# A two-block transformer layer on one core: z's projection moved into the delta rule's preparation, and the spatial mixing moved between the gates' projections

## The reference, cut to what matters

```python
mod_x = silu(c) @ ada_w + ada_b                     # six rows of 1024
hx = modulate(rms_norm(x, norm_mix_g), mod_x[0], mod_x[1])
x_qkv, x_beta, x_a, x_z, x_u, x_v, x_gates = split(hx @ w_in)   # z, u, v 1024 columns each, gates 2048
o_x = gated delta rule, both directions (x_qkv, x_beta, x_a, state of the context)
# gated_delta_chunked, for each chunk:
T = triangular_solve(eye + low, eye)                # inverse of a unit lower triangle
u = T @ (v * beta);  w = T @ (kb * exp(G))
v_new = u - w @ s;  o = q_dec @ s + qk @ v_new;  s = s * g_last + k_dec.T @ v_new
y_gdn = rms_norm(o_x, gdn_norm_g) * silu(x_z)
v = layer_norm(gelu(x_v), sgu_ln_g, sgu_ln_b)
y_sgu = gelu(x_u) * (w_s @ v + b_s)                 # 128x128 over positions, per group of 128 channels
g_a, g_b = sigmoid(x_gates)
x = x + mod_x[2] * ((g_a * (y_gdn @ w_a) + g_b * (y_sgu @ w_b)) @ w_out)
```

## Time and profile before

| | us |
|---|---|
| median of 3 timed executions | 1808.69 (1803.87 to 1810.02) |
| the profiled execution | 1803.05 |
| its span, first to last instruction | 1801.0 |
| TensorE busy in the span | 1518.5 (84%) |
| VectorE busy | 812.4 (45%) |
| ScalarE / GpSimd busy | 368.4 / 190.5 |
| mean granted clock of TensorE | 0.913 of full |

### The profile page before, as it was taken

One profiled execution on the slowest core, in us unless ns is written; L12 is line 12 of the kernel. 1 busy time (PEld: TensorE's weight loads), 2 busy tenths in 40 slices (PEclk: granted clock), 3 DMA queues, 4 the chain that ended last, 5 costly groups with the idle time before them and its releaser, 6 DMA issues. The chain is left out here.

```text
span 1801.0 us, 19500 instructions
## 1 busy us (share of the span) xinstructions
PE 1518.5 (84%) x7553; PEld 897.5 (50%) x7553; DVE 812.4 (45%) x1512; ACT 368.4 (20%) x698; POOL 190.5 (11%) x280
## 2 busy tenths in 40 slices
PE   4999964588999799465879895999889899999977
PEld 2877764578544344152324332444444447656573
DVE  2344648444254457632112114257474405566554
ACT  3221144111011100010001002100351124642230
POOL 0000016500000000001000000000251001213340
PEclk9899977567999999868989997999999999999998
DMA  9331002110677656469999995352602212121120
GB/s 350 92 94 47 1 1 48 42 34 10 234 269 264 249 215 228 154 250 419 411 384 373 411 371 174 98 182 70 187 1 70 94 47 94 47 94 47 49 70 24
DMA packets 132298, 283.60 MB, mean 157 GB/s; under 512 B 28744, under 2 KB 39272, under 8 KB 126955
## 3 DMA queue, kind: packets, MB, share of 16 engines
q1 hardware_dynamic: 128608, 266.65, 41.2%
q0 software_dynamic: 3600, 15.73, 2.1%
HBM read 312.77 MB, written 4.19 MB: 176 GB/s over the span
## 5 line engine op out<-in xcount | busy, mean ns | idle before, releaser
L1329 PE MATMUL ps<-ring,hTx 128*128 128x512 f32 x320 | 139.2, 593 | 1.9 <-PEq L176 1.8
L2641 PE MATMUL ps<-hT,ring 128*128 128x512 f32 x256 | 111.8, 593 | 3.1 <-PEq L2548 2.7
L316 DVE SCALAR_TENSOR_TENSOR ada_acc<-ring,cact,ada_acc 128x512 f32<-128x512 f32 x154 | 104.1, 745 | 0.5
L1329 PEld LDWEIGHTS ps<-ring,hTx 128*128 128x128 f32 x320 | 60.4, 190 | 77.1 <-issue 77.1
L620 PE MATMUL ps<-hTx,ring 128*128 128x256 f32 x384 | 91.1, 393 | 5.3 <-PEq L176 5.3
L2276 PE MATMUL ps<-hT,ring 128*128 128x512 f32 x208 | 90.4, 592 | 0.0
L620 PEld LDWEIGHTS ps<-hTx,ring 128*128 128x128 f32 x384 | 74.8, 197 | 19.7 <-issue 8.0
L2641 PEld LDWEIGHTS ps<-hT,ring 128*128 128x128 f32 x256 | 47.9, 190 | 60.9 <-issue 60.9
L1862 PE MATMUL ps<-ring,hTx 128*32 128x512 f32 x384 | 51.3, 683 | 26.6 <-DMA ring<-in_expert_w 26.6
L711 DVE SCALAR_TENSOR_TENSOR conv<-xpad,taps,conv 128x512 f32<-128x512 f32 (+1 forms) x96 | 63.6, 663 | 3.4
L2276 PEld LDWEIGHTS ps<-hT,ring 128*128 128x128 f32 x208 | 39.5, 190 | 48.5 <-issue 48.3
(11 more groups left out here) (522 smaller groups left out, 2680.3 us busy)
## 6 DMA issues: line engine op xcount, KB each, us to landing
ring<-in_expert_w SPq DMA_DIRECT2D x24, 2048.0 KB, 14.4
far<-in_expert_w SPq DMA_DIRECT2D x24, 2048.0 KB, 18.2
ring<-in_w_in SPq DMA_DIRECT2D x16, 2048.0 KB, 13.1
ring<-in_ada_w SPq DMA_DIRECT2D x12, 2048.0 KB, 9.2
ring<-in_w_ada SPq DMA_DIRECT2D x12, 2048.0 KB, 8.9
ring<-in_w_in_c SPq DMA_DIRECT2D x10, 2048.0 KB, 8.4
ring<-in_expert_w POOLq DMA_DIRECT2D x32, 512.0 KB
far<-in_expert_w POOLq DMA_DIRECT2D x32, 512.0 KB
```

The lines of the kernel that those rows point to most:

```text
L316: ins = dve.scalar_tensor_tensor(out=part, in0=slot[:, kt], scalar=c[:, kt:kt + 1], in1=part, op0=ALU.mult, op1=ALU.add)
L1329: ins = pe.matmul(ps[:, 2 + i % BANKS], hTx[:, kt, t * P:(t + 1) * P], stream.slot(n)[:, kt], start=(kt == 0), stop=(kt == KT - 1))
L2641: ins = pe.matmul(bank, slot[:, kt, j % 4 * P:(j % 4 + 1) * P], hT[:, kt], **edge)
```

## The change

z's two panels get a place of their own in the list, with lent panels between, and are projected in the preparation block, behind PE's last transposes; ScalarE applies Silu there, around its transposition of the solution. `zs` is allocated before the delta rule, and the state lies in `nt[:, 0]`, which is dead by then, in place of a tensor of its own. u's first panel is issued in the first scan block. In the projection stage the modulation's panels and those of `w_in` alternate from the start (eight pairs), so a modulation panel k stands in front of `w_in` panel k+1, and sum k comes behind projection k+1 as before, the last behind the last. DVE starts with the normalisation of `otok` and its product with `zs`, ahead of the first dot. The mixing block is gone: its matmuls run behind unit 12 of 16, the transposes of `otok` behind 13, those of `uu` behind 14, in banks 1, 5, 6 and 7, so the projections keep banks 2 to 4. Two lent panels behind the merge keep the experts' slots where they were. The diff, cut ("..." is left out):

```diff
-zuvg, rest = [], []
-for i in range(10):
-    zuvg.append(len(stream.panels))
+lend = lambda: add(lambda slot: [])
+z_in, gdn_lent = [], []
+for i in range(2):
+    z_in.append(len(stream.panels))
     add_cols(w_in, COL_Z + i * PANEL)
-    if 1 <= i < 9:
-        rest.append(len(stream.panels))
-        add_cols(ada, (3 + i) * PANEL)
+    for _ in range(RING - 1):
+        gdn_lent.append(len(stream.panels))
+        lend()
+uvg, rest = [], []
+for i in range(8):
+    uvg.append(len(stream.panels))
+    add_cols(w_in, COL_Z + (2 + i) * PANEL)
+    rest.append(len(stream.panels))
+    add_cols(ada, (4 + i) * PANEL)
...
+ffn_lent, ab_in = [], []
+for i in range(2):
+    ffn_lent.append(len(stream.panels))
+    lend()
...
-        state = sb(scope, "state", [P, UNITS, P])
+        state = nt[:, 0]
...
+                    stream.issue(sp, z_in[1] + 1)
                     store_solution(sp, 0)
                     load_solution(sp, 0)
...
                     turn(PAIRS - 1)
+                    pe.wait_ge(erowed, 2 * PAIRS)
+                    for i in range(2 * TT):
+                        n, t = z_in[i // TT], i % TT
+                        if t == 0:
+                            pe.wait_ge(*stream.arrive(n))
+                        for kt in range(KT):
+                            ins = pe.matmul(ps[:, i], hTx[:, kt, t * P:(t + 1) * P], stream.slot(n)[:, kt], start=(kt == 0), stop=(kt == KT - 1))
+                        ins.then_inc(z_proj, 1)
+                        if t == TT - 1:
+                            stream.free(pe, n)
...
+                    def move_z(i):
+                        act.wait_ge(z_proj, i + 1)
+                        act.activation(zs[:, i % TT, i // TT * PANEL:(i // TT + 1) * PANEL], ps[:, i], ACT.Silu)
+
                     move(PAIRS - 1)
+                    move_z(0)
+                    move_z(1)
                     turn_solution(act, 0)
+                    move_z(2)
+                    move_z(3)
...
+                        if step == 0:
+                            stream.issue(sp, uvg[0] + 1)
...
+                        if not more:
+                            for n in gdn_lent:
+                                stream.free(pe, n)
...
-        BANKS = 6
-        TURN_AT = (8, 10, 12)
-        dests = [(zs, ACT.Silu)] * 2 + [(uu, ACT.Gelu_apprx_tanh)] * 2 + [(vv, ACT.Gelu_apprx_tanh)] * 2
+        BANKS = 3
+        SGU_BANKS = (1, 5, 6, 7)
+        MIX_AT, TURN_OTOK_AT, TURN_UU_AT = 12, 13, 14
+        TURN_AT = (4, 6, 8)
+        V_DONE = 4 * TT
+        dests = [(uu, ACT.Gelu_apprx_tanh)] * 2 + [(vv, ACT.Gelu_apprx_tanh)] * 2
...
-                stream.issue(sp, zuvg[1] + 1)
+                stream.issue(sp, uvg[1] + 1)
                 sp.dma_start(spw[:, :, :], w["sgu_w"][0].rearrange("g p q -> p g q")).then_inc(loaded, 16)
                 sp.dma_start(spb_row[:, :], w["sgu_b"][0]).then_inc(loaded, 16)
                 sp.dma_start(ln_rows[:, 0], row_bcast(w["sgu_ln_g"][0])).then_inc(loaded, 16)
                 sp.dma_start(ln_rows[:, 1], row_bcast(w["sgu_ln_b"][0])).then_inc(loaded, 16)
                 sp.dma_start(gn_row[:, :], row_bcast(w["gdn_norm_g"][0])).then_inc(loaded, 16)
-                stream.issue(sp, rest[0] + 1)
                 for r in range(4):
                     sp.dma_start(mods[:, r], row_bcast(w["ada_b"][0, (2 + r) * D:(3 + r) * D])).then_inc(bias_loaded, 16)
                 stream.issue(sp, merge[0] + RING)
...
+                def mix():
+                    pe.wait_ge(v_out, 3 * TT + 1)
+                    pe.wait_ge(turned_copied, len(TURN_AT))
+                    for b in range(2 * TT):
+                        t, g0 = b // 2, 4 * (b % 2)
+                        for m in range(4):
+                            ins = pe.matmul(ps[:, SGU_BANKS[b], m * P:(m + 1) * P], spwT[:, g0 + m], vv[:, t, (g0 + m) * P:(g0 + m + 1) * P],
+                                            start=True, stop=True)
+                        ins.then_inc(mixed, 1)
+
+                def turn(src, first):
+                    pe.wait_ge(gated, 2 * TT)
+                    for b in range(KT // 2):
+                        if first:
+                            pe.wait_ge(s_moved, b + 1)
+                        transpose_in(pe, SGU_BANKS[b], lambda m: src[:, m % TT, (2 * b + m // TT) * P:(2 * b + m // TT + 1) * P], 4).then_inc(s_turned, 1)
+
+                for i in range(8 * TT):
+                    n, t = uvg[i // TT], i % TT
...
+                    if i == MIX_AT:
+                        mix()
+                    elif i == TURN_OTOK_AT:
+                        turn(otok, 0)
+                    elif i == TURN_UU_AT:
+                        turn(uu, KT // 2)
+                total(pe, 7)
...
+                    if i in (TURN_OTOK_AT, TURN_UU_AT):
+                        first = (TURN_OTOK_AT, TURN_UU_AT).index(i) * (KT // 2)
+                        for b in range(KT // 2):
+                            act.wait_ge(s_turned, first + b + 1)
+                            act.copy((ysT if first else ygT)[:, 2 * b:2 * b + 2], ps[:, SGU_BANKS[b]].rearrange("p (k t) -> p k t", k=2)).then_inc(s_moved, 1)
+                    if i == V_DONE + 1:
+                        act.wait_ge(v_step, 2 * TT)
+                        act.activation(mv[:, :, 1], mv[:, :, 1], ACT.Sqrt, bias=eps[:, 0:1]).then_inc(v_std, 1)
...
-                dve.wait_ge(bias_loaded, 64)
-                dot(dve, 0)
-
...
                 dve.wait_ge(o_step, 6)
+                dve.tensor_tensor(otok[:, :, :], otok[:, :, :], zs[:, :, :], ALU.mult)
+                dot(dve, 0)
+                dve.wait_ge(bias_loaded, 64)
                 for k in range(1, 4):
                     dot(dve, k)
                     put(dve, k - 1)
-                dve.wait_ge(moved, 2 * TT)
-                dve.tensor_tensor(otok[:, :, :], otok[:, :, :], zs[:, :, :], ALU.mult)
-                for k in range(4, 7):
-                    dot(dve, k)
-                    put(dve, k - 1)
                 for t in range(TT):
-                    dve.wait_ge(moved, 6 * TT)
+                    dve.wait_ge(moved, V_DONE)
                     for j in range(2):
                         ins = dve.bn_stats(bn[:, t, j], vv[:, t, j * 512:j * 512 + 512])
                     ins.then_inc(v_step, 1)
                     dve.wait_ge(v_step, 2 * t + 1)
                     dve.bn_aggr(mv[:, t], bn[:, t]).then_inc(v_step, 1)
-                dot(dve, 7)
-                put(dve, 6)
-                put(dve, 7)
+                dot(dve, 4)
+                put(dve, 3)
...
+                dot(dve, 5)
+                put(dve, 4)
+                for b in range(2 * TT):
+                    t, g0 = b // 2, 4 * (b % 2)
+                    dve.wait_ge(mixed, b + 1)
+                    dve.wait_ge(moved, 2 * TT)
+                    for m in range(4):
+                        g = g0 + m
+                        part = uu[:, t, g * P:(g + 1) * P]
+                        ins = dve.scalar_tensor_tensor(out=part, in0=ps[:, SGU_BANKS[b], m * P:(m + 1) * P], scalar=spb[:, g:g + 1],
+                                                       in1=part, op0=ALU.add, op1=ALU.mult)
+                    ins.then_inc(gated, 1)
+                for k in range(6, 8):
+                    dot(dve, k)
+                    put(dve, k - 1)
+                put(dve, 7)
...
+                for n in ffn_lent:
+                    stream.free(pe, n)
                 total(pe, 5)
...
```

More of the change, by code:

```diff
@@ L263, in build @@
         C_IN = len(stream.panels)
-        lend = lambda: add(lambda slot: [])
         c_panel = {}
@@ L564, in _ @@
                         sp.dma_start(rows[:, 1], row_bcast(w["dt_bias"][0].rearrange("a b -> (a b)"))).then_inc(loaded, 16)
-                        stream.issue(sp, zuvg[0] + 1)
+                        stream.issue(sp, z_in[0] + 1)
                     @block.gpsimd
@@ L775, in build @@
                 xk6 = vdec[:, :, :, :].rearrange("p a u c -> p (a u c)").rearrange("p (u c) -> p u c", c=P // 2)
-                slot_a, slot_b = (stream.slot(zuvg[0] + i).rearrange("p k n -> p (k n)") for i in (1, 2))
+                slot_a, slot_b = (stream.slot(z_in[0] + i).rearrange("p k n -> p (k n)") for i in (1, 2))
                 sc = slot_a.rearrange("p (s u c) -> p s u c", s=TT, c=P)
@@ L1311, in _ @@
                     def _(pe):
-                        for i in range(10 * TT):
-                            n, t = zuvg[i // TT], i % TT
+                        def mix():
[15 more added lines that the diff above has]
+                            n, t = uvg[i // TT], i % TT
                             if t == 0:
@@ L1352, in _ @@
                                     act.copy(spb[:, :], ps[:, 1, 0:H]).then_inc(turned_copied, 1)
-                        act.wait_ge(v_step, 2 * TT)
-                        act.activation(mv[:, :, 1], mv[:, :, 1], ACT.Sqrt, bias=eps[:, 0:1]).then_inc(v_std, 1)
```

(42 more changed lines are left out.)

10 lines of the change are left out of this document (6 added, 4 removed).

## The result

| | before | changed kernel |
|---|---|---|
| median | 1808.15 us (1803.87 to 1810.02) | 1784.71 us (1780.97 to 1786.38, 4 runs) |
| profiled execution, its span | 1803.05, 1801.0 | 1784.11, 1782.4 |

The ratio is 0.9871, with a 95% interval of 0.9847 to 0.9895: 23.4 us faster, between 19 and 28. The forecast was 32.5 us faster, 1775, with a range that reached to 1793. The time is inside it, and 10 us above the number.

A forecast was written before the change was run, and what follows sets the result against it. The gap was DVE's and SP's, with 40 us of PE idle; landing, dot, put and sum set 16 us per pair. +0.3 - 38.8 + 6 = -32.5 us gave 1770.6 to 1776.2, forecast 1775, range 1763 to 1793.

The forecast's parts named there:

- rival (a): Projection stage: late DVE makes the slot wait recur at each of six later panels, +41, 1816 us; 6%.
- Rival (b): Gap: clock stays at 1.2 GHz under the z panels, so the inverse starts 24 us late, 1799 us; 8%.
- rival (c): Front and merge hide their waits: small tensors at T0 + 15, bias rows 14 us into the merge, 1767; 20%.
- my own case: Whole kernel: the forecast's main outcome, 1769 to 1782 us; 55%.
- (d): A middling loss: some panels 1 to 2 us late, front stall 10, merge +9, 1790 us; 11%.
- Gap, +0.3: z in preparation's gap: barrier +1 to +1.6 us later, some 0.7 back in warm inverse; net +0.3, between -0.7 and +3.
- The front, T0 + 36.8 for panel 2 and a stall of 6.9: Projection stage's start: panel 2 waits for dot 0's slot, lands about T0 + 36.8; PE stalls 6.9 us, bounds 3 to 10.
- the pause in issuing: Stage's front: without it, the last small tensor was put at T0 + 18, against T0 + 19.5 for the same bytes before.
- The rest of the stage: From T0 + 36.8: 99.8 us of PE work, last put 0.7, stage end 1.6; merge at T0 + 139, -38.8.
- the 12.0 us for the block: Dealing mixing and transposes among projections: -20.9 for the stretch before the merge, +8.9 put back inside.
- The merge, +6: Bias rows queued behind two panels land 20 us into the merge, delaying merge panel 2; +6, between +1 and +9.
- the 19.8 of the estimate beside it: Merge: skill-page estimate for 8.4 MB, where the sum has 25.6; the merge would lose next to nothing.

The follow-up runs named there:

- e1_bias_later: Changed kernel with DVE's wait for the merge's bias rows moved from the merge's front to the first addition that needs them; 1776.87 us, 0.9832.
- e3_front: Changed kernel with DVE's dot 0 ahead of its small-tensor wait and the modulation's bias rows issued behind u/v panel 2; 1777.52 us, 0.9828.
- the two warm kernels: Changed kernel with 22 or 11 useless matmuls in TensorE's wait for z's second panel; 1786.0 us (22) and 1784.04 us (11).
- e7_before_bias: Kernel before, with DVE's wait for the merge's bias rows moved to the first addition that needs them; 1803.67 us, 0.9987.
- e4_u_late: Changed kernel with u's first panel issued in the third scan block instead of the first; 1784.67 us, 0.9862.
- e10_all_u_first: Changed kernel with the edits of e1_bias_later and e3_front, u's first panel issued in the first scan as in the changed kernel; 1767.4 us, 0.9784.
- e5_own_block: Changed kernel with mixing, gating and transposes back in a block of their own behind the projections, z still in the gap; 1780.56 us, 0.9852.
- e2_dot_first: Changed kernel with DVE's dot 0 put ahead of its wait for the small tensors; 1780.13 us, 0.9849.

## Why the prediction was right, and where it fell short

*The sign and the mechanism held.* TensorE had the room in the gap; the z panels went in and cost the path 1.8 us. The cycle of 16 us a pair was broken: the sums behind panels 2 to 5 follow each other in 15.1 to 15.5 us, with one stall at the front and none behind it. So rival (a) is refuted: the slack of 1.4 us was enough for all five panels behind panel 2. Rival (b) is refuted by z panel 1 in 15.02 and panel 2 in 16.63 us. What rival (c) asked for did not come by itself, but `e1_bias_later` and `e3_front` show that its two waits could be taken away, and what that is worth: 7.8 and 7.2 us, together (with u's panel moved) 17.7. The time came out between the upper end of my own case, 1782, and (d).

*Gap, +0.3, measured +3.2.* The step before the barrier was nearly right (+1 to +1.6, measured +1.8), in part by luck: the two cold starts were charged 1.9 us each and took 1.1 and 2.7. The gain in inverse 0 was larger than the 0.7 charged (1.7). What failed is that the sum had nothing for what follows: "its 2 MB delays a store that is needed 15 us later: nothing". I asked only which data the panel would hold up. In inverse 1 TensorE stops for 2.61 us, in no wait that the profile shows, while the panel is in flight.

A fetch of instructions is the likely cause of the pause. The view of the DMA queues by the microsecond has a packet of the instruction queue (0.02 MB) between 363 and 367 us in each of the nine kernels that pause there, and TensorE goes on 2 to 3.5 us behind it. In the two warm kernels the nearest in front of that place come some 10 us ahead of it (at 356 and 360 us), and they do not pause, though their panels were in flight as well. The kernel before has one such pause too, later in the program, with a packet at 393 and no bulk transfer beside it; in `e7_before_bias`, whose program for TensorE is the same, it is at another place:

```profile
396.10 0.42 PE L1049 MATMUL ps<-xk,ring 32*32 32x32 f32 x7 [0.38 <-issue]
```

```profile
433.08 0.42 PE L1049 MATMUL ps<-xk,ring 32*32 32x32 f32 x7 [0.37 <-issue]
```

Against calling it shown: the view does not say for which engine a packet is, and the kernel before has one at 363 us without a pause. That the panel lengthens the pause is not shown either. With the panel at the same place it was 3.09, 2.61, 1.25, 0.99, 0.93 and 0.91 in six kernels, with the panel elsewhere 0.67 or less in three; but the packet's share of its microsecond is 6.6 to 6.7% in the six and 6.0, 8.9 and 11.2% in the three, so the fetch is no longer behind the panel. The clock explains part of the difference: the two long pauses are in the two kernels at 0.70, where TensorE comes to that instruction sooner (2.7 us into inverse 1, in the others 3.5 to 3.6). Among the seven at 0.65, from the first matmul of inverse 1 to the end of the pause it is 4.5 to 4.8 us with the panel and 3.9 to 4.2 without, some 0.5 us. That T0 does not follow the pause's length is shown by `e4_u_late` and `e10_all_u_first`; that the clock takes the difference is what the last two windows show, but why its steps fall where they do stays open.

*The front, T0 + 36.8 for panel 2 and a stall of 6.9.* It was at T0 + 39.7, with 7.8. The small tensors came at T0 + 20.2 instead of 18, because I took away "the pause in issuing", which had cost nothing. The DMA engines are full from T0 + 2 on in either kernel: share 1.04 at 359 GB/s from 466 to 483.5 before, 1.03 at 361 GB/s from 469 to 487 now. So the same 5.8 MB took about as long, 19.5 and 20.2 us. SP needed 3.52 and 5.90 us for the issues of two small tensors behind the pair of panels, in the kernel before 0.58 and 4.44, but its slow issues left the DMA engines no idle time. The rest is the landing, 8.9 and not 8.2. Not counted at all was the cold start behind the stall, 15.52 us for a panel of 13.90, though the gap's own step had charged 1.9 for just that. The wait for panel 1 was 1.54 us, where the forecast had 1, and the 1.23 at sum 0 come out of dot 0's lateness.

*The rest of the stage,* T0 + 39.7 to 144.5, is 104.8 where the sum had 102.2: 1.6 are that cold panel, and the six gaps of 0.26 us before the sums cover the rest. The booking was wrong though: of the 12.0 us for the block, 10.2 came without any dealing (`e5_own_block`).

*The merge, +6, measured +8.7.* The bias rows landed 19.4 us into the merge, as forecast to within a microsecond, and the wait before merge panel 2 was 6.64 us, as the forecast's "about 6". By the Trainium skill ("DMA: Bandwidth & Descriptors", "Queues, rings and completion order") each DMA engine takes a queue's descriptors in the order of its ring and increments the semaphore behind all its earlier writes, so that the rows can't be there before the panels in front of them. This trace agrees: the panels, issued at 606.74 and 607.33, land 8.6 and 13.9 us later; x and the two rows, issued at 611.71, 612.12 and 612.81, land 12.0, 15.3 and 18.4 us later, in that order. From 606.74 to the last row it is 24.4 us, near the 25.6 of the sum and not the 19.8 of the estimate beside it. The missing 2.7 us are nearly all once more a panel that starts cold, 16.50 for 13.9. So a wait of 6 to 9 us was under-priced twice, by 1.6 and by 2.6: the wait was right and its price was not.

*Behind the merge* the profiles give back 2.7 us of the 21.3, the timed medians nothing. From the start of the routing to the end of the span it is 1050.3 us before, 1053.0 in the changed kernel, and between 1047.5 and 1055.8 in the kernels of the experiments, whose instructions there are the same. That spread has no cause here that a run isolates.

## What to carry to other kernels

When work leaves a stage, list the transfers that its slack had covered and price each at its new place, with the cold panel behind each wait: here two short waits took about 17 of the 40 us that the change had opened. Before dealing a block's work out among other work, ask what the block waits for: here it was one square root at the end of ScalarE's program, 10 of the 12 us came without the dealing, and a plain block behind the projections did as well as the dealt one. In a chain "transfer, work of an engine, free slot, transfer", whatever stands in front of that engine's work at the head of the chain (a small tensor, a bias row) delays a 2 MB load that does not need it.

## What the runs showed of the hardware

- After a wait of 6.6 to 9.2 us TensorE's next panel took 15.5 to 16.6 us for 13.9, at each of the changed kernel's three long waits. Shorter waits did it too: 5.31 us in `e2_dot_first` (15.81), and 2.13 in `e1_bias_later` (15.70, with the granted clock at 0.62 and 0.53 in the first two stretches of 2 us behind it). It need not be so: after 1.54 us the changed kernel's panel took 14.00, and after 2.56 us of idling the kernel before took 28.07 for two. Filling the wait with other matmuls takes the cost away (13.90 in both warm kernels), at no gain if something else ends last.
- TensorE can stop in the middle of a group, in no wait that the profile shows, for 0.35 to 3.1 us. In nine kernels with z in the gap it is at one and the same instruction; in the kernel before and in `e7_before_bias`, with the same program for TensorE, it is at two different ones (396.10 and 433.08).
- SP's issue of a DMA lengthens behind two 2 MB panels: 3.52 and 5.90 us for two small tensors, 0.58 and 4.44 behind one panel in the kernel before. The DMA engines were full meanwhile (share 1.05 from 471 to 487).
- The granted clock over small matmuls differs from kernel to kernel with identical instructions (0.65 and 0.70 in inverse 1 and scan 1, with 0.73 in the kernel before), and the stretch from the last addition to T0 with it, 142.1 to 142.4 or 145.0 to 145.4 us. A gain of 2 us in front of such a stretch can't be read from the end of it.
